# The latents' norms by token columns: sums, roots and inversions of 4 or 8 columns, spread over the rows by TensorE, in place of 128x512 fields

## What is computed

```python
y_ssm = rmsnorm(y_ssm, g[:D_SSM])                      # one norm per token over 512 channels
y_conv = rmsnorm(y_conv.reshape(bn, seq_len, 8, 64), g[D_SSM:].reshape(8, 64))   # per token and head of 64
y = concatenate([y_ssm, y_conv]) @ p["w_out"]
x = x + g1 * y
h = rmsnorm(x, p["norm2_g"]) * (1 + sc2) + sh2         # one norm per token over 1024 channels
x = x + g2 * peer(h, ...)                              # 8 heads x 16 experts per token
```

## Time and profile before

| what | us |
|---|---|
| median of 3 runs | 1967.68 (1967.2 to 1967.95) |
| the profiled execution | 1977.83 |
| its span in the trace | 1976.0 |

### The profile page before, as it was taken

One profiled execution on the slowest core, in us unless ns is written; L12 is line 12 of the kernel. 1 busy time (PEld: TensorE's weight loads), 2 busy tenths in 40 slices (PEclk: granted clock), 3 DMA queues, 4 the chain that ended last, 5 costly groups with the idle time before them and its releaser, 6 DMA issues.

```text
span 1976.0 us, 22252 instructions
## 1 busy us (share of the span) xinstructions
PE 1196.6 (61%) x7540; PEld 460.7 (23%) x7540; DVE 1441.2 (73%) x3894; ACT 375.7 (19%) x845; POOL 719.9 (36%) x666
## 2 busy tenths in 40 slices
PE   6999888988767666775544434464434454444444
PEld 3569533333323222221101000021000011011001
DVE  8977566877766776666788777777777777876765
ACT  5232431221222111111221011121111111211110
POOL 0000332333333433433443444444344444344442
PEclk9999998999878777776655555565555566555555
DMA  8556799999989999999999999999999999999996
GB/s 347 173 202 227 279 367 344 377 376 387 396 330 384 389 397 388 397 403 372 420 417 421 421 414 416 420 407 419 413 413 419 410 413 410 416 417 411 414 417 255
DMA packets 126242, 745.90 MB, mean 377 GB/s; under 512 B 12128, under 2 KB 34912, under 8 KB 40624
## 3 DMA queue, kind: packets, MB, share of 16 engines
q0 software_dynamic: 92160, 671.13, 83.2%
q1 hardware_dynamic: 33968, 73.35, 10.4%
HBM read 741.78 MB, written 2.65 MB: 377 GB/s over the span
## 4 chain that ended last, share of the span: by engine, by line
DMA 34%; PE 29%; DVE 24%; issue 10%; ACT 1%; SPq 0%; DVEq 0%; POOL 0%; POOLq 0%; ACTq 0%
DMA r<-table,gidx 30%; DVE r L1678 8%; PE bank L846 7%; PE bank L814 6%; DMA r<-w_query 3%; PE bank L923 3%; PE bank L934 2%; PE bank L543 2%; DMA r<-w_u 2%; DVE wgt L1690 1%; PE bank L781 1%; DVE r L1646 1%; DVE i L1620 1%; DVE i L1626 1%; DVE r L1621 1%
## 5 line engine op out<-in xcount | busy, mean ns | idle before, releaser
L1861 POOL DMA_INDIRECT r<-table,gidx x640 | 711.7, 1112 | 1072.8 <-PE bank L846 911.2
L1678 DVE CUSTOM_DVE_ANT_0 r<-r 128x1024 f32<-128x1024 f32 x640 | 780.0, 1224 | 302.7 <-DMA r<-table,gidx 273.9
L846 PE MATMUL bank<-r,wgt 128*32 128x512 f32 x2560 | 536.0, 923 | 729.3 <-DVE wgt L1690 710.5
L846 PEld LDWEIGHTS bank<-r,wgt 128*32 128x32 f32 x2560 | 61.5, 131 | 1103.4 <-DVE wgt L1690 1033.6
L1228 ACT ACTIVATE r<-r 128x2 f32<-128x2 f32 x320 | 65.1, 203 | 1046.5 <-DVE r L1678 1038.6
L814 PE MATMUL bank<-hT_r,r 128*128 128x512 f32 x256 | 123.6, 639 | 0.9 <-ACT hT_r L1082 0.9
L1687 DVE TENSOR_TENSOR r<-r 128x2 f32<-128x2 f32 x320 | 50.1, 157 | 92.3 <-ACT r L1228 92.3
L1690 DVE TENSOR_TENSOR wgt<-fold,r 128x64 f32<-128x64 f32 x320 | 72.0, 225 | 11.1
L814 PEld LDWEIGHTS bank<-hT_r,r 128*128 128x128 f32 x256 | 51.3, 206 | 77.6 <-issue 77.6
L1228 ACT ACT_TABLE_LOAD x51 | 65.4, 1283 | 0.9
L923 PE MATMUL bank<-hT_r,r 128*128 128x512 f32 x128 | 62.2, 631 | 0.0
(11 more groups left out here) (356 smaller groups left out, 1431.4 us busy)
## 6 DMA issues: line engine op xcount, KB each, us to landing
r<-w_mod SPq DMA_DIRECT2D x24, 1024.0 KB, 8.4
r<-w_query SPq DMA_DIRECT2D x15, 1024.0 KB
r<-table,gidx POOLq DMA_INDIRECT x640
r<-w_tiles SPq DMA_DIRECT2D x12, 512.0 KB, 6.7
x_r<-w_tiles SPq DMA_DIRECT2D x10, 512.0 KB, 5.8
hT_r<-xT SPq DMA_DIRECT2D x4, 640.0 KB, 6.2
r<-w_u SPq DMA_DIRECT2D x1, 2048.0 KB, 30.5
r<-w_o SPq DMA_DIRECT2D x1, 2048.0 KB, 11.1
```

The source lines that it names most:

```text
L846: last = mm(bank[ACC[b % 2][h]][to:to + TG, :], wgt[:, g % 2, e, :], rows[:, k % SLOTS, D + h * 512:D + (h + 1) * 512], start=(G % HEADS = ...
L1678: V.tensor_tensor_reduce(rows[:, s, 0:D], rows[:, s, 0:D], h2r[tg], 1.0, 0.0, ALU.mult, ALU.add, hid[:, par, k:k + 1]).then_inc(dot_done, 1)
L1861: G_.indirect_dma_start(rows[:, k % SLOTS, :], None, table, bass.IndirectOffsetOnAxis(gidx[:, e, k:k + 1], 0)).then_inc(row_in[k % SLOTS], 16)
```

## The change

The squares become the stationary operand, token block by token block, and a column of ones (or two columns of `headones`) moves: the sums then stand as columns, tokens on the partitions, 4 columns (4 x 128 tokens) or 8 (times two heads). Root and inversion are made of these columns. A new function on PE, `spread_columns`, multiplies each column, broadcast over 128 (or 64) columns as the stationary operand, with the identity, which puts the inverse into all rows of `bank[6]`, and DVE's multiplications read the bank. `rsl` goes; the columns lie in free places of `frs`.

```diff
+        rtl, invl = ([frs[:, c + (8 * w - 4 if w else 0):c + (8 * w + 4 if 0 < w <= KS else 8 * w - 4 * (w > KS) + 4)] for w in range(KS + 2)] for c in (32, 80))
@@ PE
+            def column_sums(squares, first, final):
+                for j in range(4):
+                    last = mm(bank[6][:, j:j + 1], squares[:, j * P:(j + 1) * P], ones[:, 0:1], start=(first and j == 0), stop=final,
+                              skip_group_check=True)
+                last.then_inc(sql_used, 1)
+            def spread_columns(w):
+                pe.wait_ge(inv_ready, 4 + w)
+                for j in range(4):
+                    tokens = slice(j * P, (j + 1) * P)
+                    if w in (0, KS + 1):
+                        last = mm(bank[6][:, tokens], invl[w][:, j:j + 1].broadcast_to([P, P]), ident[:, :], start=True, stop=True)
+                    else:
+                        for h in range(2):
+                            last = mm(bank[6][64 * h:64 * h + 64, tokens], invl[w][:, 2 * j + h:2 * j + h + 1].broadcast_to([P, 64]), ident[:, :],
+                                      start=True, stop=True)
+                last.then_inc(inv_mm, 1)
-                    mm(bank[6][:, :], ones[:, :], sql[n % 2], start=(n == 4), stop=(n == 7)).then_inc(sql_used, 1)
+                    column_sums(sql[n % 2], n == 4, n == 7)
+                if n == 9:
+                    spread_columns(0)
+                if n in (13, 19, 25, 31):
+                    spread_columns((n - 7) // 6)
+                if n == 47:
+                    spread_columns(KS + 1)
@@ PE, n in (12, 18, 24, 30)
-                    pe.wait_ge(rms_l, i + 1)
-                    mm(bank[6][:, :], headones[:, :], sql[i % 2], start=True, stop=True).then_inc(sql_used, 1)
+                    pe.wait_ge(mixl_ready, i + 1)
+                    for j in range(4):
+                        last = mm(bank[6][:, 2 * j:2 * j + 2], sql[i % 2][:, j * P:(j + 1) * P], headones[:, 0:P:64], start=True, stop=True)
+                    last.then_inc(sql_used, 1)
@@ ACT (the other two roots likewise, of 4 columns)
-                        act.wait_ge(mixl_ready, 1 + i)
-                        A(rsl, bank[6][:, :], ACT.Sqrt, scale=1.0 / (DC // 8), bias=eps_c[:, 0:1]).then_inc(rms_l, 1)
+                        A(rtl[1 + i], bank[6][:, 0:8], ACT.Sqrt, scale=1.0 / (DC // 8), bias=eps_c[:, 0:1]).then_inc(rms_l, 1)
@@ DVE
-                if n == 10:
-                    dve.wait_ge(rms_l, 1)
-                    ll(V.reciprocal(rsl, rsl))
+                for w, at in enumerate((9, 14, 20, 26, 32, 48)):
+                    if n == at:
+                        dve.wait_ge(rms_l, w + 1)
+                        V.reciprocal(invl[w], rtl[w]).then_inc(inv_ready, 1)
                 if n == 11:
                     dve.wait_ge(glul_ev, KS)
+                    dve.wait_ge(inv_mm, 4)
                     for m in range(KS):
-                        last = stt(mixl[:, m, :], mixl[:, m, :], col(COL_OG + m), rsl, ALU.mult, ALU.mult)
+                        last = stt(mixl[:, m, :], mixl[:, m, :], col(COL_OG + m), bank[6][:, :], ALU.mult, ALU.mult)
@@ DVE, n == c + 11
-                        dve.wait_ge(rms_l, 2 + i)
-                        ll(V.reciprocal(rsl, rsl))
+                        dve.wait_ge(inv_mm, 5 + i)
                         dve.wait_ge(cbl_ev, i + 1)
-                        stt(mixl[:, KS + i, :], mixl[:, KS + i, :], col(COL_OG + KS + i), rsl, ALU.mult, ALU.mult).then_inc(mixl_ready, 1)
+                        stt(mixl[:, KS + i, :], mixl[:, KS + i, :], col(COL_OG + KS + i), bank[6][:, :], ALU.mult, ALU.mult).then_inc(mixl_ready, 1)
```

More of the change, by code:

```diff
@@ L961, in latent_front @@
                     if m == 0:
-                        pe.wait_ge(rms_l, 5)
+                        pe.wait_ge(mixl_ready, KS + 1)
                     pe.wait_ge(sql_ready, 9 + m)
-                    mm(bank[6][:, :], ones[:, :], sql[m % 2], start=(m == 0), stop=(m == KD - 1)).then_inc(sql_used, 1)
+                    column_sums(sql[m % 2], m == 0, m == KD - 1)
             def last_rows(n):
@@ L1286, in latent_front @@
                     act.wait_ge(sql_used, 4)
-                    A(rsl, bank[6][:, :], ACT.Sqrt, scale=1.0 / DS, bias=eps_c[:, 0:1]).then_inc(rms_l, 1)
+                    A(rtl[0], bank[6][:, 0:4], ACT.Sqrt, scale=1.0 / DS, bias=eps_c[:, 0:1]).then_inc(rms_l, 1)
                 for i in range(KS):
@@ L1305, in latent_front @@
                     act.wait_ge(sql_used, 2 * KD)
-                    A(rsl, bank[6][:, :], ACT.Sqrt, scale=1.0 / D, bias=eps_c[:, 0:1]).then_inc(rms_l, 1)
+                    A(rtl[KS + 1], bank[6][:, 0:4], ACT.Sqrt, scale=1.0 / D, bias=eps_c[:, 0:1]).then_inc(rms_l, 1)
                 if 50 <= n < 53:
@@ L1759, in latent_front @@
                 if n == 49:
-                    dve.wait_ge(rms_l, 6)
-                    ll(V.reciprocal(rsl, rsl))
+                    dve.wait_ge(inv_mm, KS + 5)
                     dve.wait_ge(x1l_ready, KD)
@@ L1764, in latent_front @@
                     k = slice(3 * (n - 49), min(3 * (n - 49) + 3, KD))
-                    tt(hT[:, k, CTX:T], xtl[:, k, :], rsl.rearrange("p (a t) -> p a t", a=1).broadcast_to([P, k.stop - k.start, LAT]),
+                    tt(hT[:, k, CTX:T], xtl[:, k, :], bank[6][:, :].rearrange("p (a t) -> p a t", a=1).broadcast_to([P, k.stop - k.start, LAT]),
                        ALU.mult).then_inc(xsl_ready, 1)
```

1 line of the change is left out of this document (removed).

## The result

The changed kernel took 1958.7 us in the median (1955.36 to 1962.83, 8 runs), against 1967.82 (8 runs) of the kernel before on the same chip. The ratio is 0.9942 with the 95% interval [0.9926, 0.9958]; a second timing of both kernels gave 0.9936 [0.9913, 0.9958]. By the medians that is a gain of 9.1 us and, the second time, of 11.9; by the ratios it is 11.4 and 12.6 us of some 1970, where 15.6 had been forecast. The profiled execution took 1956.29 us, its span 1954.5.

The account below looks back on a forecast made before the run. In the mixer PE and DVE take turns as the bound, later the row gathers. 5.3 + 3.35 + 5.8 + 3.15 - 2.0 = 15.6 us gained, so 1967.7 becomes 1952.1 us; range 1946 to 1963.5.

Parts of the forecast that it names:

- A: Step 10: weights come earlier without the wide reciprocal, 2.7 us, and PE's full clock returns, 2.6; gain 5.3 us.
- B: Step 15: PE's 3.50 us wait lies all behind the wide reciprocal; gain 3.35 us.
- E: Step 33: 3.35 us less the narrow inversion's 0.20, plus PE's clock back, 0.87 + 1.80; gain 5.8 us.
- F: Step 49: PE waits 8.02 us on busy DVE; 3.35 less 0.20, gain 3.15 us, PE's clock staying low.
- C: Step 21: PE reaches the next add_rows without a wait, so PE bounds; gain 0.
- D: Step 27: the query weights' transfer ends PE's 2.96 us wait whatever DVE does; gain 0.
- rival 3: More than counted: clock holds at step 27, shortening query and add_rows, likewise behind 560 us; about 4 more, 1948; chance 0.08.
- Spreads: Six new PE spreads of 1.02 us; only those at n = 13 and 19 cost time, minus 2.0 us.
- Narrow sums: Sixteen column sums replace sixteen wide ones on PE; gain of at most 1.1 us, counted as nothing.
- Rival 4: Slower by the clock: 22 narrow groups may cost 2.6 us each, slower from the fifth; eight give 1978; chance 0.06.
- Rival 1: Inversions go but the clock stays low at steps 10 and 33; gain 10.3 us, 1957.4; chance 0.24.
- Rival 2: DMA takes over as DVE's 4.2 us row waits grow; 5 us of gain stay, 1962.7; chance 0.13.

Follow-up runs that it names:

- filler: The kernel before plus seven wide matmuls nobody reads, where PE idled at steps 9, 10 and 32; 1963.81 us, ratio to before 0.9968.
- best: The changed kernel with third and fourth norms wide again and the second norm's spread moved behind step 14's scores; 1954.51 us, ratio to before 0.9907.
- warm: best plus eight small unread matmuls ahead of three add_rows in each of seven latent-query head groups; 1947.07 us, ratio to before 0.9882.
- warm_more: warm with the small unread matmuls ahead of add_rows at g = 0 too; 1950.33 us, ratio to before 0.99.
- spread_twice: The changed kernel with every spread issued twice, the second over the first with the same values; 1959.79 us, ratio to before 0.9941.

## Why the prediction was right, and where it was off

The side, the range and the mechanism held: 1958.7 lies between 1946 and 1963.5. Of the 15.6 us of the sum the three pairs of kernels gave 9 to 13 by their medians and 11 to 13 by their ratios. Term by term, with what every execution shows apart from what chance adds:

- **The inversions, A, B, E, F**: "the weights come 3.35 earlier". They measured 3.2, 3.3, 3.3 and 3.3 us at steps 10, 15, 33 and 49, in each kernel that has them, and nothing at C. A's was priced at 2.7, because PE would not be ready sooner; the others came as forecast. B and E were never tested alone.
- **A's clock, 2.6** and **E's, 2.67**: this is the step that failed. I put down to the change all that the half clock cost in one execution of before. The filler shows the mechanism right; but A's drop costs nothing in one of five executions with the wide norm, and still costs 1.7 us in two of eight with the narrow one, so A's clock is worth 1.9 - 0.7 = 1.2 on the mean. At E, from step 34 to 38, the narrow ones gain 1.6 to 2.6 us, mean 2.4, the wide ones without filler between a loss of 0.3 and a gain of 1.0, mean 0.2: net 2.2. There PE's wait ahead of the weights shrank from 4.26 us to 0.93, and the clock held:

```profile
441.73 1.07 PE L846 MATMUL bank<-r,wgt 128*32 128x512 f32 x8 [0.93 <-DVE wgt L1719]
442.73 2.84 PE L964 MATMUL bank<-mix_r,r 128*128 128x512 f32 x6
```

- **D, 0 forecast**: 3.1 at step 27 in the kernel after, of which the ten kernels without a narrow D get some at step 29 (0 to 3.2, mean 1.9). Net 1.2. The wait for the query weights shrank from 2.96 to 1.48 us and the query behind it from 3.39 to 2.05. That looks like rival 3's first half, but six of the ten kernels with a wide D have 2.05 too, behind waits of 1.37 to 2.62 us, so it can't be put down to D; what makes it in them was not found. D was never tested alone.

```profile
407.27 2.05 PE L781 MATMUL bank<-hT_r,r 128*128 128x128 f32 x16 [1.48 <-DMA r<-w_query]
```

- **Spreads, -2.0**: -1.0 at n = 13 and -1.1 at n = 19 as priced, but -1.1 at n = 25 too, where "PE's waits at 412.69" were to cover it: weights in between had to be made later before PE came to that wait. And 0.7 us more at step 19, which the prediction lacks. PE now waits ahead of step 16 alone, 2.82 us, where in before it waited 3.50 ahead of step 15 and 1.12 ahead of step 16. In after the clock falls there, in `best` it does not:

```profile
341.17 1.24 PE L846 MATMUL bank<-r,wgt 128*32 128x512 f32 x8 [2.82 <-DVE wgt L1719]
342.34 5.17 PE L951 MATMUL bank<-hT_r,mix_r 128*128 128x512 f32 x8
```

```profile
335.90 1.06 PE L849 MATMUL bank<-r,wgt 128*32 128x512 f32 x8 [2.82 <-DVE wgt L1743]
336.89 3.70 PE L959 MATMUL bank<-hT_r,mix_r 128*128 128x512 f32 x8
```

  The five executions with this half clock (the three of after, warm, warm_more) lose 0.7 or 0.8 us at step 19, the two that have the wait and not the half clock (best, spread_twice) lose nothing.
- **Narrow sums, 0**: "at most 1.1 us" of gain, taken as zero. They are as long as the wide ones (16 records 1.84 against 4 of 1.88), but the clock drop at step 39 costs 1.6. Rival 4 was right in mechanism in one of its 22 groups, and the fifth never came; `PEclk` over 240 to 525 is 0.96, where before had 0.95 over 240 to 530. The window that I had named as a sign of being wrong reads 0.89, under the 0.9 that I had set:

```profile
480.00:515.00 35.00, 34.51 (x186) 17.10 (x186) 24.37 (x63) 6.02 (x14) 12.56 (x12) 1.00 1.00 390
480.00:530.00 50.00, 42.90 (x228) 20.69 (x227) 38.39 (x107) 11.87 (x25) 19.57 (x19) 0.89 1.01 400
```

  Up to 515 us, where the narrow sums lie between wide work, it is 1.00. The low part is the idle end of the mixer, which now starts 15 us earlier and falls into the window, and the drop at step 39 lies ahead of it. So the sign came for a reason that it was not made for.
- **New waits, 0**: 0.8 us for the spread, 9.4 for the root beside busy PE. Right.

Together 13.1 + 1.2 + 2.2 + 1.2 - 3.2 - 0.7 - 1.6 = 12.2 us, less the 1.0 that may be lost behind step 116: 11.2 us, where the three pairs of kernels, by their ratios, give 11.4, 12.6 and 13.0 (1970 times the difference). The mixers of these pairs differ by 14.8 on the mean; 2.3 of the 2.6 us over the sum lie at steps 13, 29 and 34 to 38, where these six executions differ by more than the means above, and six can't tell that from chance. Nor do the kernels with one norm alone bear out the terms by their run times (1.8 us for A, 6.9 for F). So the total is measured, the inversions are shown at their steps, and how the rest divides is an estimate. Rival 1 had 10.3 and the forecast 15.6; the truth lies between, as the clock came back in part.

**Rival 2**, DMA taking it over, did not show as a loss at the end, though its sign did: DVE waited 17.2 us for rows, and 14.4 to 19.8 in all three executions. I had said that waits far over 4.2 would speak against the forecast. From step 40 to 46 they cost the path nothing: the shift goes from -12.4 to -12.5 while five of these waits pass. The longer ones, up to 3.2 us between 452 and 472, lie where the shift falls back from -13.5 (step 35) to -10.6 (37) and is at -14.1 again at step 38. Whether a further gain in the mixer would still reach the end with the DMA share at 0.99 stays open; `best` points that way, but not beyond the noise.

What I had promised of the profile: DVE's busy time fell by 18.0 us (forecast 19), PE's rose by 0.5, PE's wait ahead of step 15 went whole, its wait for the query weights at D stayed in part, and after steps 10 and 33 the wide groups took their full-clock 3.70 (eight records) and 2.84 (six). At F:

```profile
533.65 1.93 PE L846 MATMUL bank<-r,wgt 128*32 128x512 f32 x8 [4.69 <-DVE wgt L1719]
```

8.02 us of waiting became 4.69, 3.33 less.

## What to carry to other kernels

Price an inversion (or any work of DVE) by the wait that stands behind it on PE: four of six were worth their full 3.3 us at their step, the fifth nothing and the sixth about 1 us, and three of the six spreads cost their length. Count half-clock stretches from one trace only at their mean over several executions: here the one profile of before held 2.6 us of them at step 10, which another execution of the same code there did not have to pay, and up to 3 us at step 29. And where PE idles in a steady pattern, cheap work that nobody reads can be worth more than a rewrite: 24 small matmuls in each of seven head groups gave 8.5 us in the kernel before by its ratio (5.7 to 11.0 by the interval), 8.9 in the kernel after (0.9936 to 0.9891) and 5 in `best`.
